# Moving the modulation chunks of a three-layer network to other places of the program, and changing how they are summed and how the row scans are made

## The reference

```
mod = silu(c) @ w_mod[layer] + b_mod[layer]                  # 1024 -> 6 * 1024
sh1, sc1, g1, sh2, sc2, g2 = jnp.split(mod, 6, axis=-1)
mod_c = silu(c_ctx) @ w_mod[layer] + b_mod[layer]            # the same for the context
h  = rmsnorm(x) * gain * (1 + sc1) + sh1
x  = x + g1 * mixer(h)                                       # layer 1: gated delta rule, short conv, Fourier mix
h2 = rmsnorm(x) * gain2 * (1 + sc2) + sh2                    # layer 2: retention and mLSTM
x  = x + g2 * swiglu(h2, w_ffn_in, w_ffn_out)                # layer 3: windowed attention with a sink
```

## Time and profile before

| | us |
|---|---|
| runs, median of 3 | 2188.15 (2186.59 to 2191.15) |
| profiled execution, its own time | 2180.8 |
| its span | 2178.9 |
| PE busy | 1936.7 |
| mean granted clock of PE | 0.946 |

### The profile page before, as it was taken

One profiled execution on the slowest core, in us unless ns is written; L12 is line 12 of the kernel. 1 busy time (PEld: TensorE's weight loads), 2 busy tenths in 40 slices (PEclk: granted clock), 3 DMA queues, 4 the chain that ended last, 5 costly groups with the idle time before them and its releaser, 6 DMA issues.

```text
span 2178.9 us, 31030 instructions
## 1 busy us (share of the span) xinstructions
PE 1936.7 (89%) x12948; PEld 1671.0 (77%) x12948; DVE 1099.7 (50%) x1831; ACT 776.2 (36%) x1322; POOL 473.1 (22%) x224
## 2 busy tenths in 40 slices
PE   4989898988878999989888985899999988798999
PEld 2777687877767889878767983688888867478999
DVE  2668323555545343354578786422222244984443
ACT  3444423222224355532053212332222233465443
POOL 0112121223212233421111000122222222003443
PEclk8999999999899999999898996999999999799999
DMA  7446365332224665522021000222222223003553
GB/s 301 177 153 246 141 248 217 117 109 86 78 78 181 257 234 186 174 78 78 10 78 58 20 1 4 74 97 97 97 97 95 79 87 117 0 1 135 194 194 136
DMA packets 36570, 262.05 MB, mean 120 GB/s; under 512 B 4048, under 2 KB 4176, under 8 KB 6224
## 3 DMA queue, kind: packets, MB, share of 16 engines
q1 hardware_dynamic: 36432, 260.07, 32.9%
HBM read 259.00 MB, written 1.05 MB: 119 GB/s over the span
## 4 chain that ended last, share of the span: by engine, by line
PE 70%; DVE 17%; DMA 5%; ACT 4%; issue 3%; POOL 2%; SPq 0%; DVEq 0%; ACTq 0%; POOLq 0%
PE ps L727 15%; PE ps L729 15%; PE ps L728 15%; PE ps L777 3%; PE ps L968 2%; PE ps L980 2%; PE ps L986 2%; DMA raw<-in_w_gate 2%; PE ps L754 2%; PE ps L794 2%; POOL wl L644 1%; ACT wh L1270 1%; PE ps L823 1%; DVE msq L2173 1%; PE ps L1170 1%
## 5 line engine op out<-in xcount | busy, mean ns | idle before, releaser
L644 POOL TENSOR_TENSOR wl<-raw,wh 128x1024 fp32r<-128x1024 f32 (+1 forms) x165 | 392.5, 2379 | 1459.8 <-ACT wh L1270 1459.7
L727 PE MATMUL ps<-h_hi,wh 128*128 128x256 f32 (+1 forms) x1696 | 549.9, 324 | 21.5 <-POOL wl L644 16.6
L729 PE MATMUL ps<-h_hi,wl 128*128 128x256 f32 (+1 forms) x1696 | 542.5, 320 | 0.0
L1270 ACT ACTIVATE wh<-raw 128x1024 fp32r<-128x1024 f32 (+1 forms) x330 | 342.6, 1040 | 560.3 <-PE ps L729 304.8
L728 PE MATMUL ps<-h_lo,wh 128*128 128x256 f32 (+1 forms) x1696 | 541.0, 319 | 0.0
L1739 DVE TENSOR_TENSOR wl<-raw,wh 128x1024 fp32r<-128x1024 f32 (+1 forms) x165 | 223.0, 1351 | 282.1 <-ACT wh L1270 262.3
L727 PEld LDWEIGHTS ps<-h_hi,wh 128*128 128x128 f32 x1696 | 320.3, 189 | 49.9 <-POOL wl L644 19.6
L728 PEld LDWEIGHTS ps<-h_lo,wh 128*128 128x128 f32 x1696 | 320.3, 189 | 26.5 <-issue 1.2
L729 PEld LDWEIGHTS ps<-h_hi,wl 128*128 128x128 f32 x1696 | 320.0, 189 | 25.9
L727 PE MATMUL ps<-gh,wh 128*128 128x256 f32 (+1 forms) x528 | 171.5, 325 | 1.2 <-POOL wl L644 1.2
L729 PE MATMUL ps<-gh,wl 128*128 128x256 f32 (+1 forms) x528 | 166.9, 316 | 0.0
(11 more groups left out here) (416 smaller groups left out, 3201.4 us busy)
## 6 DMA issues: line engine op xcount, KB each, us to landing
raw<-in_mod SPq DMA_DIRECT2D x72, 1024.0 KB, 5.3
raw<-in_ffn_in SPq DMA_DIRECT2D x66, 1024.0 KB, 4.8
raw<-in_ffn_out SPq DMA_DIRECT2D x24, 1024.0 KB, 4.8
raw<-in_w_in SPq DMA_DIRECT2D x16, 1024.0 KB, 4.8
raw<-in_w_gate SPq DMA_DIRECT2D x12, 1024.0 KB, 4.8
raw<-in_w_ab SPq DMA_DIRECT2D x12, 1024.0 KB, 4.8
raw<-in_ffn_out SPq DMA_DIRECT2D x12, 768.0 KB, 4.2
raw<-in_w_at SPq DMA_DIRECT2D x5, 1024.0 KB, 4.7
```

The costliest lines, as they stand in the source:

```text
L644: nc.gpsimd.tensor_tensor(wl[e % SPLIT][:, 0:entries[e]["words"]], part(e), wh[e % SPLIT][:, 0:entries[e]["words"]].bitcast(F32), ALU.subt ...
L727: nc.tensor.matmul(b[:, cols], wh[e % SPLIT][:, w], xh(k), start=(k == 0), stop=False)
L729: ins = nc.tensor.matmul(b[:, cols], wl[e % SPLIT][:, w], xh(k), start=False, stop=(k == nk - 1))
L1270: A(wh[e % SPLIT][:, 0:x["words"]], part(e), ACT.Copy).then_inc(hi_ready, 1)
```

## The change

The calls of `mod()` are put elsewhere. The 9 and 6 of the start stay. The 10 in z to fn, the 12 in the gates, the 24 in the levels of the delta scan and the 12 in the first feed-forward part go. Of these 58 calls, in their new places:

- 16 stand in the prologues of the four delta steps: two ahead of the first `X0T`, one ahead of the second, one behind `KQ`, which now stands behind the `X0T` tiles;
- 2 behind `oss`, 2 behind `ydn`, 2 at layer 1's second norm (a2);
- 3 ahead of the first pair of layer 2 (`rq`, norm b1), 3 in the retention ahead of `RB`, 4 around the sums `mss` of the mLSTM heads, 3 at norm b2;
- 3 ahead of the first pair of layer 3 (`ak`, norm c1), 9 in the loop over the query heads' sums `aqss`, 3 at norm c2;
- 8 remain beside dense work: 7 in the second feed-forward part (`sprinkled`) and 1 in the third.

In the plan, `load` places the next stage's first weight chunk ahead of these calls and `use` its tiles behind them. `modcol` is now two matmuls with `modrow` as the stationary operand and a table `pick` of two columns as the moving one, so PE sums the four parts and DVE's summing instruction goes. `cst` goes: the conditioning vector in `small` is passed through silu in place and is the stationary operand. `scan_dve` becomes eight `tensor_tensor_scan` instructions of 32x128. On ACT and DVE some `ahead` calls move: DVE's split of `z` 3 from the middle of the scan to behind it, those of the first feed-forward tiles to behind the norm, that of `wo` to ahead of the calls at `ydn`.

```diff
+def sprinkled(nm, j):
+    return {"1": (2, 4, 8, 10, 14, 18, 20), "2": (2,)}.get(nm, ()).count(j)
...
+    def load(name, i, keys):
+        chunk(name, i)
+        for key in keys:
+            entry(KD * P, [key])
+    def use(keys):
+        for key in keys:
+            add(*key)
+            entries[entry_of[key]]["last"] = len(tile) - 1
...
             for j in range(k0, k0 + nk):
-                split("ffn_in" + name, j, [("fa" + name, j), ("fb" + name, j)])
-                if sprinkle:
-                    mod()
+                if j == 0:
+                    load("ffn_in" + name, 0, [("fa" + name, 0), ("fb" + name, 0)])
+                    mod(2 if name == "0" else 3)
+                    use([("fa" + name, 0), ("fb" + name, 0)])
+                else:
+                    split("ffn_in" + name, j, [("fa" + name, j), ("fb" + name, j)])
+                mod(sprinkled(name, j))
...
         if j >= 8:
             add("l2", j - 8)
-        mod()
...
             split("w_gate", 4 * b + j, [(gate, 2 * j), (gate, 2 * j + 1)])
-            mod()
...
             add("GR", n)
             add("KK", n)
+        for n in two:
+            mod(2 - n % 2)
+            add("X0T", n)
+        for n in two:
             if s >= 2:
                 add("KQ", n)
-        for n in two:
-            add("X0T", n)
+        mod()
         for lv in range(1, LV):
             for n in two:
                 add("Y", n, lv)
-            mod()
             for n in two:
                 add("ZT", n, lv)
...
     add("oss", 0)
     add("oss", 1)
+    fence()
+    load("w_o", 0, [("wo", 0), ("wo", 1)])
+    mod(2)
     for j in range(2):
         chunk("w_dn_out", j)
         direct([("ydn", 4 * j + i) for i in range(4)])
-    fence()
-    for j in range(4):
+    mod(2)
+    use([("wo", 0), ("wo", 1)])
+    for j in range(1, 4):
         split("w_o", j, [("wo", 2 * j), ("wo", 2 * j + 1)])
     norm("a2")
-    ffn("0", True, "b1c")
+    ffn("0", "b1c")
     norm("b1")
-    for j in range(4):
+    load("w_ab", 0, [("rq", 0), ("rq", 1)])
+    mod(3)
+    use([("rq", 0), ("rq", 1)])
...
         if s > 0:
+            mod()
             add("RB", s)
         add("RO", s)
...
+    load("w_abo", 0, [("abo", 0), ("abo", 1)])
+    mod(2)
+    add("mss", 0)
+    add("mss", 1)
+    mod()
+    add("mss", 2)
+    add("mss", 3)
+    mod()
+    use([("abo", 0), ("abo", 1)])
...
+    load("w_at", 4, [("ak", 0), ("ak", 1)])
+    mod(3)
+    use([("ak", 0), ("ak", 1)])
...
+    for i in range(9):
+        if i < 8:
+            add("aqss", i)
+        mod()
         if i > 0:
             add("aqsw", i - 1)
...
-    def scan_dve(dve, link, bufs, final, op, done, midway=None):
+    def scan_dve(dve, src, dst, op, start, done):
         V = nc.vector
-        cur = bufs[0]
-        step = 1
-        i = 0
-        while step < CH:
-            nxt = final if 2 * step >= CH else bufs[(i + 1) % 2]
-            for d in range(2):
-                rr = slice(32 * d, 32 * d + 32)
-                x = cur[rr, :].rearrange("p (c t) -> p c t", c=NC)
-                y = nxt[rr, :].rearrange("p (c t) -> p c t", c=NC)
-                if d == 0:
-                    V.tensor_tensor(y[:, :, step:], x[:, :, step:], x[:, :, 0:CH - step], op)
-                    V.tensor_copy(y[:, :, 0:step], x[:, :, 0:step])
-                else:
-                    V.tensor_tensor(y[:, :, 0:CH - step], x[:, :, 0:CH - step], x[:, :, step:], op)
-                    ins = V.tensor_copy(y[:, :, CH - step:], x[:, :, CH - step:])
-            if 2 * step >= CH:
-                ins.then_inc(sem(done), 1)
-                dve.wait_ge(sem(done), 1)
-            else:
-                link(ins)
-            if midway and step == 8:
-                midway()
-            cur = nxt
-            step *= 2
-            i += 1
+        for d in range(2):
+            rr = slice(32 * d, 32 * d + 32)
+            turn = 1 if d == 0 else -1
+            for c in range(NC):
+                tk = slice(CH * c, CH * c + CH)
+                ins = V.tensor_tensor_scan(dst[rr, tk][:, ::turn], CA("ones")[rr, :], src[rr, tk][:, ::turn], start,
+                                           ALU.mult, op)
+        ins.then_inc(sem(done), 1)
+        dve.wait_ge(sem(done), 1)
...
                 for k in range(KD):
                     j = k % 4
-                    ins = nc.tensor.matmul(b[32 * j:32 * j + 32, 0:256], cst[:, min(n // 24, 1), k, :],
+                    o = SMALL["cvec"][0] + 16 * min(n // 24, 1) + 2 * k
+                    ins = nc.tensor.matmul(b[32 * j:32 * j + 32, 0:256], small[:, o:o + 32],
                                            w[:, 256 * k:256 * k + 256], start=(k < 4), stop=(k >= 4),
                                            skip_group_check=True)
                 close(ins)
...
                 evacuated(pe, "modrow", n - 1)
                 b = begin("modcol", n - 1)
                 for i in range(2):
-                    ins = nc.tensor.transpose(b[:, P * i:P * i + P], modrow[:, (n - 1) % 2, P * i:P * i + P], ident)
+                    ins = nc.tensor.matmul(b[:, 2 * i:2 * i + 2], modrow[:, (n - 1) % 2, P * i:P * i + P], S("pick"),
+                                           start=True, stop=True)
                 close(ins)
...
-                dst = mods[:, lay, 2 * c:2 * c + 2, :]
-                link(V.tensor_reduce(dst, bank("modcol", n)[:, 0:256].rearrange("p (m j v) -> p m v j", m=2, j=4)
-                                     [:, :, 0:2, :], AX.X, ALU.add))
-                o = 48 * lay + 2 * c
...
+                    free(V.tensor_tensor(mods[:, lay, 2 * c:2 * c + 2, :],
+                                         bank("modcol", n)[:, 0:4].rearrange("p (m v) -> p m v", m=2), bias,
+                                         ALU.add), "modcol", n)
...
-        ahead("z", 1)
-        scan_dve(dve, link, (rows[0:64, 0, :], rows[0:64, 1, :]), RM[0:64, :], ALU.add, "RM_ready",
-                 lambda: ahead("z", 3))
+        scan_dve(dve, rows[0:64, 0, :], RM[0:64, :], ALU.add, 0.0, "RM_ready")
...
             V.tensor_tensor(o, o, zsave[:, 2 * i:2 * i + 2, :], ALU.mult).then_inc(sem("ydn_in"), 2)
+        ahead("wo", 0, depth=2)
+        mod(2)
```

More of the change, by code:

```diff
@@ L296, in make_plan @@
     add("aksw", 1)
-    for i in range(8):
-        add("aqss", i)
+    load("w_ato", 0, [("ato", 0), ("ato", 1)])
+    for i in range(9):
+        if i < 8:
+            add("aqss", i)
+        mod()
         if i > 0:
             add("aqsw", i - 1)
-    add("aqsw", 7)
     for u in range(-1, 16 + 2):
```

263 lines of the change are left out of this document (139 added, 124 removed).

## The result

The changed kernel takes 2095.72 us, median of 4 runs (2091.39 to 2098.31), against 2187.37 us of before in the same comparison: a ratio of 0.9585, 95% interval 0.9558 to 0.9612. Its profiled execution took 2094.28 us. It answers to the 2180.8 us on which the sum was made: -86.5 us by the trace, where -73.5 was forecast.

The account below looks back on a forecast made before the run. PE, busy 89%, was taken as the bound, so calls should move from dense stages into its waits. Terms summed to -73.5 us: 2180.8 to 2107.3 profiled, plus 7.35 for a median of 2114 us, range 2088 to 2144.

Parts of the forecast that it names:

- Gates: Three gates: twelve calls of 1.28 us go, with all 6.35 us of PE gaps; about -22 us, at least -15.4.
- First feed-forward part: First feed-forward part: twelve calls (15.4 us) go, with gaps of 6.0 us; -21.4 us, at least -15.4.
- z to fn: Stretch z to fn: ten calls and 4 us of gaps go, against later DVE split of z 3; -14 us.
- Delta scan: Delta scan: 24 calls leave the levels (-30.7 us), each latent step loses 4 us; -22.7 us, from -31 to -15.
- oss, ydn, wo: From `oss` to `wo`: `ydn` starts 6.4 us later behind split and transfer; +4.2 us at `wo`, from -2.2 to +9.
- Clock: Filled waits restore PE's clock: -3 us over six norms, -5.2 in the retention, 1.7 of the mLSTM start's -4.7.
- Calls beside dense work: Dense work: eight calls come at 1.28 us, +10.2 us, and their `modcol` products add +1.9 us.
- A: Rival: the waits are not empty, 2 us late at each of 14 places, 28 us lost; 2142 us, chance 0.17.
- C: Rival: slower, as each of 50 calls exposes part of its chunk's transfer; at 2 us each 2214 us, chance 0.03.
- D: Rival: transfers bound the dense stages, so their 57.4 us of gains don't show; 2186 us, chance 0.01.
- B: Rival: PE's clock holds through norms and retention, and z to fn loses its gaps; 2095 us (2085 to 2100), chance 0.19.
- main case: The whole kernel: the summed terms hold, giving a median of 2100 to 2130 us; chance 0.60.

Follow-up runs that it names:

- the recurrences alone: Kernel before with only its doubling scans replaced by the eight `tensor_tensor_scan` instructions: 2183.64 us, ratio 0.9992.

## Why the prediction was right, and where it was off

- **What bounds the kernel** was right: the waits went and PE's work stayed, and the calls put back in the gates cost what they had cost.
- **The price of a call** was sized too low, 1.28 us. A level of the scan shows 1.37, and in the gates PE's busy time fell by 18.2 us for twelve calls, 1.51 each. That is 2.2 us of the delta scan's difference and the 2.4 of the gates'.
- **Gates.** The mechanism holds, all gaps out included (-24.4 for -22).
- **First feed-forward part.** -22.8 for -21.4 is right in part by luck. The gaps went, but the window of the earlier trace rows holds ten chunks of modulation and not twelve (the trace has 160 matmuls from L777 in it, 16 for each chunk), and 3.1 us of the measured gain are the spacing of matmuls (720 of them, 0.0043 us each), which the prediction didn't have.
- **z to fn.** -17.2 for -14, again not by the terms as they stood. I kept DVE as a second bound and took 4 of 7.1 us of gaps; PE lost its calls' 10 us but only 1.0 of gaps in that window, and stands idle 6.1 now. What made up for it lies behind the window, 6.3 us between 233 and 254, on a path that the prediction didn't have. The timelines of ACT and PE in the kernel before, and of PE in the changed one:

```profile
237.65 1.06 ACT L1270 ACTIVATE wh<-raw 128x1024 fp32r<-128x1024 f32 x1 [4.41 <-DMA raw<-in_w_gate]
241.36 9.79 PE L899 MATMUL ps<-const,fch 128*128 128x256 f32 x32 [4.18 <-ACT fch L1447]
228.54 7.17 PE L927 MATMUL ps<-const,fch 128*128 128x256 f32 x32 [0.49 <-ACT fch L1478]
```

  Before, ACT had a split to make ahead of `fch`, and its chunk of `w_gate` was only issued at 232.8, when a modulation chunk had been used. ACT waited 4.41 us for it and PE 4.18 us for `fch`, and PE then ran these products at a mean granted clock of 0.72 (9.6 us, now 7.0 at 1.00). With no modulation between them the chunks of `w_gate` are now issued from 206.9 on, well ahead: 3.7 us of wait and 2.6 of clock.
- **Delta scan.** Right in size (-25.0 for -22.7, the difference being the price of a call) and in kind: the context prologues are free. The 4 us for a latent step were 4.7 and 3.3 against the kernel without calls, and the cause is the one named, ACT's and DVE's queues: an order alone took 4.1 and 4.0 away.
- **oss, ydn, wo.** +4.8 for +4.2; the delay of `ydn` by split and transfer is shown. That it could be had back cheaply isn't: the call behind `ydn` was the next late thing.
- **Clock.** The term of the retention was right in size (4.8 for 5.2) but not as it was made up. Two stages at full clock were taken; one came to it (2.5 us), and the two behind it gave 0.8 and 1.4. Other kernels with the same calls have other stages at full clock. The five norms gave some 6.5 us where 1.3 was taken: 2.4 up to the start of the pair, where the calls were to cost 1.7, and 4.1 inside the pairs, where 3 was taken for the clock. The price of a wait is its length and a few us of half speed behind it; so the latent step gained 4.0 us for 3.1 of wait, and the mLSTM 3.6 more than its 3.0 of wait. There I had taken 1.7, and that term was mis-sized (-4.7 for -6.6).
- **Calls beside dense work.** +11.6 for 7 calls in the second part, 1.66 each for 1.52. Of the 1.66, 0.27 are the product with `pick`, so the call of before would be 1.39. In levels (1.64) and in the first feed-forward part (1.6) the price is the same.
- **What no step had**: the spacing of 256-column matmuls. It gave about 5 us in the first part (3.1 of them inside the table's window) and took 6 in the third, so it nearly cancels in the result, but not in the experiments.
- **Rivals.** A, C and D fell with the run without the calls and the one with twelve back in the gates. The median of 2095.72 lies in B's 2085 to 2100 and below the main case's 2100 to 2130. But B had only half of the mechanism: the clock did come back, from 0.946 to 0.966, though not through all of the retention; z to fn kept most of its gaps, and other terms carried as much of the difference.
- The forecast is 18 us above the median. 13 of them are the terms (-73.5 for -86.5). The other 5 to 6 are that a median 7.35 us above the profiled execution was taken over from before, where the changed kernel has 1.4.

## What to carry to other kernels

Work that nobody waits for costs its full engine time in a dense stage and next to nothing in a wait of the same engine, if its data is there, its bank free and its readers on the other engines not queued behind what the wait is for. Look for the last of these first: the calls of the latent steps, which cost about 4 us each time, stood behind an addition that another engine did too late, and an order repaired it. And count the wait together with the slow stretch behind it: here a wait that was filled early mostly saved more than its length, and work that was put at the end of a long one ran at half speed. Look, too, at what the moved work leaves behind: in a ring of three slots a chunk that nobody waits for held up one that ACT's queue stood behind.

## What the runs showed of the hardware

- Matmuls with 256 moving columns, without a gap and at granted clock 1.00, follow each other either in 0.1134 or in 0.1177 us, for stretches of more than a thousand. Which of the two a stretch gets is fixed by the program as far as one repetition shows (the same kernel twice: the same 1079 matmuls), and changes with edits hundreds of us away: the recurrences alone moved the last part of the kernel before from 0.113 to 0.118, which cost 6.1 us and hid what they had gained. What sets it stays open.
- A wait of 2.45 us ahead of `RB` is followed by 5.3 us of work at clock 0.50 in three kernels, and by 3.34 us at 0.82 in a fourth; a wait of 0.92 us by 2.78 us at 1.00 in most kernels and by 5.28 us at 0.50 in one. The length of the last wait doesn't tell it alone.
